# The last sixteen gate tiles of an input projection as eight pairs of seven block products

## The reference

```python
u = x @ w_in[l]
ua, ub, uc, ug = _split(u, GROUP_COLS)
oa, oc = _gdn_branch(ua, ...), _swa_branch(uc, ...)
ob, v_first = _rwkv7_branch(ub, x, ...)
gates = jax.nn.sigmoid(ug).reshape(bsz, t, N_BRANCH, d)
merged = (gates[:, :, 0] * (oa @ w_branch_a[l]) + gates[:, :, 1] * (ob @ w_branch_b[l])
          + gates[:, :, 2] * (oc @ w_branch_c[l]))
x = _layer_norm(ALPHA * x + merged @ w_out[l], ln1_w[l], ln1_b[l])
hid = jax.nn.silu(x @ ffn_gate[l]) * (x @ ffn_up[l])
x = _layer_norm(ALPHA * x + hid @ ffn_down[l], ln2_w[l], ln2_b[l])
```

## Time and profile before

| | us |
|---|---|
| median of 3 runs | 1847.23 (1846.68 to 1847.53) |
| the profiled execution, its own time | 1851.59 |
| its span | 1849.8 |
| PE busy | 1811.3 |
| DVE busy | 1139.0 |
| ACT busy | 670.3 |
| POOL busy | 591.2 |
| granted clock, mean | 0.992 |

### The profile page before, as it was taken

The page is one execution under the profiler, slowest core; times in us unless marked ns, Lnnn a source line. Parts: engine busy times, 40 slices in busy tenths (PEclk is TensorE's granted clock), DMA queues, the critical chain, the costliest instruction groups (busy, mean ns, idle before and its releaser), DMA issues. The chain is left out here.

```text
span 1849.8 us, 28784 instructions
## 1 busy us (share of the span) xinstructions
PE 1811.3 (98%) x11396; PEld 1488.5 (80%) x11396; DVE 1139.0 (62%) x1347; ACT 670.3 (36%) x1140; POOL 591.2 (32%) x420
## 2 busy tenths in 40 slices
PE   7999999999999999999989999999999999999997
PEld 6878888777788888788878778888888888888885
DVE  3757675666309940377768653966566666565586
ACT  3444434244421112266652131243333333444241
POOL 1211222211123322344415452765555554500000
PEclk9999999999999999999999999999999999999998
DMA  6245675225673377377755473234545445488563
GB/s 175 49 88 136 150 183 140 73 73 145 164 199 92 93 164 223 115 214 222 206 191 191 132 236 109 82 98 154 189 135 157 151 163 185 150 277 301 179 213 132
DMA packets 383030, 292.76 MB, mean 158 GB/s; under 512 B 170764, under 2 KB 314764, under 8 KB 380848
## 3 DMA queue, kind: packets, MB, share of 16 engines
q1 hardware_dynamic: 307472, 237.14, 43.4%
q10 hardware_dynamic: 75424, 53.78, 10.4%
HBM read 195.84 MB, written 94.98 MB: 157 GB/s over the span
## 5 line engine op out<-in xcount | busy, mean ns | idle before, releaser
L158 PE MATMUL bank<-xhi,w_hi 128*128 128x512 f32 x976 | 385.8, 395 | 5.8 <-POOL w_lo L446 2.7
L160 PE MATMUL bank<-xhi,w_lo 128*128 128x512 f32 x976 | 381.0, 390 | 0.0
L159 PE MATMUL bank<-xlo,w_hi 128*128 128x512 f32 x976 | 380.5, 390 | 0.0
L446 POOL TENSOR_TENSOR w_lo<-w_raw,w_hi 128x1024 fp32r<-128x1024 f32 x61 | 169.2, 2774 | 572.2 <-ACT w_hi L813 572.2
L158 PEld LDWEIGHTS bank<-xhi,w_hi 128*128 128x128 f32 x976 | 183.6, 188 | 47.8 <-issue 7.3
L160 PEld LDWEIGHTS bank<-xhi,w_lo 128*128 128x128 f32 x976 | 183.5, 188 | 39.4
L159 PEld LDWEIGHTS bank<-xlo,w_hi 128*128 128x128 f32 x976 | 183.8, 188 | 37.0
L1931 POOL TENSOR_TENSOR ff_ring_lo<-ff_w_sums,ff_ring_hi 128x512 fp32r<-128x512 f32 x88 | 127.6, 1451 | 73.7 <-ACT ff_ring_hi L2210 73.5
L1931 POOL TENSOR_TENSOR ff_ring_lo<-ff_raw,ff_ring_hi 128x512 fp32r<-128x512 f32 x66 | 95.9, 1455 | 149.6 <-ACT ff_ring_hi L2210 149.5
L799 ACT ACTIVATE work<-bank 128x512 f32<-128x512 f32 x70 | 42.0, 600 | 264.1 <-PE bank L160 256.3
L165 PE MATMUL b_ps<-x1hi,ff_ring_hi 128*128 128x512 f32 x264 | 103.0, 390 | 0.0
(11 more groups left out here) (410 smaller groups left out, 3984.1 us busy)
## 6 DMA issues: line engine op xcount, KB each, us to landing
w_raw<-in_w_in ACTq DMA_DIRECT2D x61, 512.0 KB, 4.4
hid_ops<-y SPq DMA_DIRECT2D x77, 256.0 KB, 2.8
ff_raw<-hid_ops SPq DMA_DIRECT2D x77, 256.0 KB, 3.8
op<-opnd SPq DMA_DIRECT2D x16, 1152.0 KB, 5.5
u<-work ACTq DMA_DIRECT2D x68, 256.0 KB, 4.3
b_gate<-u SPq DMA_DIRECT2D x24, 512.0 KB, 4.0
ff_raw<-in_ffn_gate SPq DMA_DIRECT2D x22, 512.0 KB, 4.2
ff_raw<-in_ffn_up SPq DMA_DIRECT2D x22, 512.0 KB, 6.0
```

What stands on the lines that cost most here:

```text
L158: pe.matmul(out, w_hi, x_hi, start=first, stop=False)
L159: pe.matmul(out, w_hi, x_lo, start=False, stop=False)
L160: return pe.matmul(out, w_lo, x_hi, start=False, stop=last)
L446: pool.tensor_tensor(w_lo[b][:, :, :], w_raw[b][:, :, :], as_f32(w_hi[b][:, :, :]), ALU.subtract).then_inc(w_lo_done, 1)
```

## The change

The last 16 of the 61 tiles, all of them gates, are no longer computed tile by tile. They form eight pairs; a pair with the two halves of the channels and the two halves of the frames is a 2x2 by 2x2 block product, done by Winograd's form of Strassen's method in seven products of blocks in place of eight. A product is 4 channel blocks by three matmuls of 128x512.

- The seven products take sums of blocks. Sums of the tokens are made once (`t1` to `t4`, four blocks each): two of them by POOL between the last seven ordinary tiles, one by DVE before the pairs' fifth product, one by DVE near the end. Each sum is split again into a high part (ACT) and a low part. Sums of the weights are made by POOL for every pair (`pair_sum`), and a high and a low part for each of the products (`pair_high` on ACT, `pair_low` on POOL).
- Six products of each pair come one after the other (`PAIR_ORDER`), their sums accumulate in PSUM or are added by DVE (`add_u2`, `add_rest`); the partial result that waits for the seventh goes to a DRAM buffer `hold` or stays in SBUF. The seventh products of all pairs follow as a second pass (`second`), with `last_add` on DVE. Sigmoid and store are ACT's.
- Both raw tiles of a pair have one buffer; the next pair is loaded (`load_pair`) when the third low part of the pair is done.
- The inversion starts with the RWKV blocks alone, 44 steps, while the last GDN blocks are still on their way; then the parts alternate. Between its steps stand DVE's sums for the pairs, at fixed step numbers (`STEPS_BEFORE`).
- Before the scan only chunks 0 and 1 are loaded; chunk 2 is loaded at the beginning of the scan, since its tiles' space is used for token sums.

The core of the diff (8 columns of indentation cut off):

```diff
-    NT_IN = len(ORDER)
+    NT_IN = len(ORDER) - 2 * PAIRS
     NQ = 2 * NT_IN
-    at_tile = {row: m for m, row in enumerate(ORDER)}
+    G, NP1 = PAIRS, 6 * PAIRS
+    PAIR_ORDER = (1, 6, 2, 7, 5, 3)
+    SECOND = (G - 2, G - 1, *range(G - 2))
...
+t1 = [x_of(k, 1) for k in range(4)]
+t2 = list(zip(in_raws[0:4], (*in_raws[4:6], t2_low_up[:, :], t2_turned[:, :])))
+t3 = [(pieces(t3_tile, HALF * k), pieces(t3_tile, HALF * (4 + k))) for k in range(4)]
...
+x_part = {1: [x_of(k, 0) for k in range(4)], 2: [x_of(4 + k, 0) for k in range(4)], 3: [x_of(4 + k, 1) for k in range(4)],
+          4: t2, 5: t1, 6: t2, 7: t3}
+w_slot = lambda w, n: w[(NT_IN + n % 4 // 2) % 2][:, n % 2 * 4:n % 2 * 4 + 4, :]
...
-inv_n, inv_x, inv_xt, prod = of_blocks(8), of_blocks(11), of_blocks(0), of_blocks(14)
+inv_n, inv_x, inv_xt, prod = of_blocks(8), of_blocks(11), of_blocks(8), of_blocks(14)
 R = NPAIR // 2
 PARTS = (slice(0, 2), slice(2, R))
-INV_STEPS = 2 + 2 * (NB - 1)
+INV_STEPS, ALONE = 2 + 2 * (NB - 1), 44
+STEPS_BEFORE = (70, 72, 76, 78, 86, 88, 104, 106, 115, 117, 123, 125)
...
+    def sum_t2(k):
+        out, (bh, bl), (dh, dl), (ah, al) = t2_sum[k], x_of(k, 1), x_of(4 + k, 1), x_of(k, 0)
+        if k == 0:
+            pool.wait_ge(conv_done, 12)
+        if k == 3:
+            pool.wait_ge(turn_stored[0], 16 * turn_count[0])
+        step(pool.tensor_tensor(out, as_f32(dh), as_f32(bh), ALU.subtract))
...
+        summed(pool.tensor_tensor(out, out, as_f32(al), ALU.add), ("t sum", k))
...
+    def sum_t3(k):
+        out, (th, tl), (ah, al) = t3_sum[k], t2[k], x_of(k, 0)
+        if k == 0:
+            for b in range(2):
+                pool.wait_ge(g_stored[b], 96)
+            pool.wait_ge(mm_done, max(turned_by("gdn", i, n) for i in range(GH) for n in "vk"))
+            pool.wait_ge(sums_made, made["t lo", 3])
...
+    def pair_sum(g, p):
+        a11, a12 = (flat4(raw_of(0, kh)) for kh in range(2))
+        a21, a22 = (flat4(raw_of(1, kh)) for kh in range(2))
+        a, b, how = {5: (a21, a22, ALU.add), 6: (s_sums[5], a11, ALU.subtract), 7: (a11, a21, ALU.subtract), 3: (a12, s_sums[6], ALU.subtract)}[p]
+        if p == 5:
+            pool.wait_ge(p_landed, 32 * g + 48)
+        if g:
+            pool.wait_ge(w_lo_done, NT_IN + 6 * (g - 1) + PAIR_ORDER.index(p) + 1)
+        if p == 6:
+            pool.wait_ge(sums_made, made["weight", g, 5])
+        if p == 3:
+            pool.wait_ge(sums_made, made["weight", g, 6])
+        summed(pool.tensor_tensor(s_sums[p], a, b, how), ("weight", g, p))
...
+    first = NT_IN - 7
+    sums = {first: [(sum_t2, 0)], first + 1: [(sum_t2, 1), (low_t, 0)], first + 2: [(sum_t2, 2), (low_t, 1)], first + 3: [(sum_t2, 3), (low_t, 2)],
+            first + 4: [(low_t, 3), (sum_t3, 0), (sum_t3, 1)], first + 5: [(low_t, 4), (low_t, 5), (sum_t3, 2), (sum_t3, 3)], first + 6: [(low_t, 6), (low_t, 7)]}
     for m in range(NT_IN):
         b = m % 2
         pool.wait_ge(w_hi_done, m + 1)
         pool.tensor_tensor(w_lo[b][:, :, :], w_raw[b][:, :, :], as_f32(w_hi[b][:, :, :]), ALU.subtract).then_inc(w_lo_done, 1)
+        for do, k in sums.get(m, ()):
+            do(k)
+    for g in range(G):
+        if g == 0:
+            pair_sum(0, 5)
+            pair_sum(0, 6)
+        n = 6 * g
+        pair_low(n)
+        pair_low(n + 1)
+        pair_sum(g, 7)
+        pair_sum(g, 3)
+        for k in range(2, 5):
+            pair_low(n + k)
+        if g + 1 < G:
+            pair_sum(g + 1, 5)
+            pair_sum(g + 1, 6)
+        pair_low(n + 5)
+    for i in range(G):
+        pair_low(NP1 + i)
...
+            else:
+                sp.wait_ge(nt_stored, 480)
+                for r in range(2):
+                    for pp in range(2):
+                        sp.dma_start(inv_n[64 * pp:64 * pp + 64, r, :, :], nt[2 * r + pp].rearrange("c b s t -> (c b) s t")).then_inc(inv_landed, 16)
...
+    load_chunk(sp, 0, early, opnd, xinv, early_landed, early_inv)
+    sp.wait_ge(early_landed, 112)
+    sp.wait_ge(early_inv, 48)
+    sp.wait_ge(p_held, 16 * (G - 1))
+    sp.wait_ge(w_lo_done, NT_IN + NP1)
+    sp.wait_ge(p_add, add_at(G - 1, 3))
+    for i in range(2, 5):
+        sp.dma_start(second_piece[i], hold[SECOND[i]]).then_inc(p_back, 16)
+    sp.wait_ge(p_add, add_at(G - 1, 5))
+    sp.dma_start(second_piece[5], hold[SECOND[5]]).then_inc(p_back, 16)
+    sp.wait_ge(mm_done, N_MM + NP1)
+    load_chunk(sp, 1, early, opnd, xinv, early_landed, early_inv)
...
+    def product(n):
+        g, p = n // 6, PAIR_ORDER[n % 6]
+        to = pair_bank[g % 2][X_AT[p]]
+        pe.wait_ge(w_lo_done, NT_IN + n + 1)
+        if p == 1:
+            if g == 0:
+                pe.wait_ge(g_norm_done, GH)
+                pe.wait_ge(masked, 16)
+            elif g == 1:
+                pe.wait_ge(evac, len(ITEMS))
+            else:
+                pe.wait_ge(p_read, snap_at(g - 2) + 1)
+        elif p == 2:
+            pe.wait_ge(p_read, snap_at(g))
+        elif p == 6 and g >= 2:
+            pe.wait_ge(p_add, add_at(g - 2, 5))
+        elif p == 3:
+            pe.wait_ge(p_add, add_at(g, 1))
+        for k in range(4):
+            if g == 0 and p in (6, 7):
+                pe.wait_ge(sums_made, made["t lo", 4 * (p - 6) + k])
+            if g == 0 and p == 5:
+                pe.wait_ge(p_add, edge_lo_at(0, k))
+            last = more_dot(pe, to, w_slot(w_hi, n)[:, k, :], w_slot(w_lo, n)[:, k, :], *x_part[p][k], p != 2 and k == 0)
+        last.then_inc(mm_done, 1)
...
+    def high_t1(k):
+        act.wait_ge(p_add, edge_sum_at(0, k))
+        act.activation(t1[k][0], t1_sum[k], ACT.Copy).then_inc(t_hi, 1)
...
+    def load_pair(g):
+        act.wait_ge(w_lo_done, NT_IN)
+        if g:
+            act.wait_ge(w_lo_done, NT_IN + 6 * g - 3)
+        for i in range(2):
+            col = in_column(gate_row(g, i))
+            act.dma_start(w_raw[i][:, :, :], w_rows[:, :, col:col + P]).then_inc(p_landed, 16)
...
+    high_after = {2 * (NT_IN - 6 + k): (k,) for k in range(4)}
+    high_after[NQ - 4], high_after[NQ - 2] = (4, 5), (6, 7)
...
+            for n in high_after.get(q, ()):
+                high_t(n)
+            if q == NQ - 3:
+                load_pair(0)
+            if q >= NQ - 2:
+                pair_high(q - (NQ - 2))
     store_u(NQ - 2)
+    high_t1(0)
     finish(NQ - 1)
+    pair_high(2)
     store_u(NQ - 1)
+    high_t1(1)
+    pair_high(3)
...
+    for j in range(NP1 + G):
+        act.wait_ge(mm_done, N_MM + j + 1)
+        g, p = j // 6, PAIR_ORDER[j % 6]
+        if j < NP1:
+            if p == 1:
+                act.activation(snap, pair_bank[g % 2][0], ACT.Copy).then_inc(p_read, 1)
+                if g + 1 < G:
+                    load_pair(g + 1)
+            if p == 2:
+                pair_out(g, 0)
+        if j + 4 < NP1 + 4:
+            pair_high(j + 4)
+        elif NP1 < j < NP1 + G - 3:
+            pair_high(j + 3)
+        if j < 2:
+            high_t1(j + 2)
...
+    def make_t1(_):
+        dve.wait_ge(mm_done, done_at[NQ - 2])
+        dve.wait_ge(sums_made, made["t sum", 3])
+        for k in range(4):
+            out, (hi, lo), (ah, al) = t1_sum[k], t1[k], x_of(k, 0)
+            step(dve.tensor_tensor(out, as_f32(lo), as_f32(al), ALU.subtract))
+            step(dve.tensor_tensor(out, out, as_f32(hi), ALU.add))
+            dve.tensor_tensor(out, out, as_f32(ah), ALU.subtract).then_inc(p_add, 1)
+            if k:
+                low_t1(k - 1)
...
+    def add_u2(g):
+        if g:
+            dve.wait_ge(p_add, add_at(g - 1, 5))
+        dve.wait_ge(mm_done, N_MM + 6 * g + 2)
+        dve.wait_ge(p_read, snap_at(g))
+        dve.tensor_tensor(u2, pair_bank[g % 2][1], snap, ALU.add).then_inc(p_add, 1)
...
+    todo = [(make_t1, 0)]
+    for g in range(G):
+        todo += [(add_u2, g)] + ([(make_t4, 0)] if g == G - 1 else []) + [(add_rest, g)]
+    todo += [(last_add, i) for i in range(G)]
+    parts, done, turn_at = [steps(part) for part in PARTS], [0, 0], list(STEPS_BEFORE)
+    for n, k in enumerate((0,) * ALONE + (1, 0) * (INV_STEPS - ALONE) + (1,) * ALONE):
+        while turn_at and turn_at[0] <= n:
+            turn_at.pop(0)
+            do, at = todo.pop(0)
+            do(at)
+        if done[k]:
+            dve.wait_ge(inv_step[k], done[k])
+        else:
+            dve.wait_ge(inv_landed, (64, 32 * R)[k])
+        next(parts[k]).then_inc(inv_step[k], 1)
+        done[k] += 1
...
+            for u_stored, count in u_last:
+                sp.wait_ge(u_stored, count)
+            load_chunk(sp, 2, tiles, opnd, xinv, landed[2], inv_landed[2])
```

More of the change, by code:

```diff
@@ L316, in project_and_prepare @@
     raw_use, seen = {}, [0, 0, 0]
-    for row in ORDER:
+    for row in ORDER[:NT_IN]:
         if row in RAW_SLOT:
@@ L402, in project_and_prepare, with summed @@
         inv_step = [sem(f"inv_step{k}") for k in range(2)]
-        block = local.open_block()
```

(69 more changed lines are left out.)

226 lines of the change are left out of this document (185 added, 41 removed).

## The result

The changed kernel takes 1895.24 us (median of 4 runs, 1894.26 to 1896.27), the kernel before 1846.95 beside it: 1.0266 times as long, interval 1.0253 to 1.0279. That is 48.3 us more where +32.7 was forecast, and less than half a microsecond beyond the range (1847.2 x 1.0266 = 1896.4, the range ended at 1896). The sign was right, and it lies where the forecast put it; the size was not right.

What follows compares the result with a forecast made beforehand. PE bounds the old kernel; after the change, POOL and DVE's serial chain holds PE. 782.6 + 1.2 + 6 + 2.3 - 759.4 = +32.7 us, on 1847.2 gives 1880 us; range 1837 to 1896 for 8 in 10.

Steps and rivals of the forecast that it cites:

- Matmuls, 21.8 us saved: Last sixteen tiles on PE: 672 matmuls in place of 768, at 0.2267 us each, 21.8 us less.
- POOL and DVE exclude each other: Projection: POOL sums and DVE instructions with two SBUF inputs run one after the other, whole instruction by whole instruction.
- The serial sum, 199.3 us from 518, and 6 idle: Until the sixth pair's second product: POOL's 122.1 plus DVE's 77.2 us run serially, to 717.3; about 6 us with neither running.
- Clock at 0 in a chain that POOL holds: PE's lower clock after stalls, mostly covered by POOL's chain: taken as 0, at most 2.5 us in each of five stalls.
- After 717.3 come 24 products, 65.3 us, and two load loops 1.2: From the sixth pair's second product to PE's end: 65.3 us of products plus 1.2 us for weight loads, nothing else.
- rival D: PE's clock drops in each stall uncovered: forecast plus 12, 1892 us; chance counted within the forecast's 0.68.
- Inversion's way out at nothing: Inversion's stores and chunk 0's load after its end near 728 us: done ahead of PE's 790, no cost.
- Boundary 2.3: From PE's last product to the scan: DVE add, four memsets, ACT's sigmoid and store beside them, 2.3 us.
- A: Rival: POOL late only by its own work, DVE's work falling into POOL's waits: 9.1 us gained, 1838 us; chance 0.13.
- C: Rival: half of the POOL and DVE collisions count, 38.6 us instead of 77.2: 1840 to 1862 us; chance 0.11.
- B: Rival: PE stays the bound and everything is hidden: 19.5 us gained, 1828 us; chance 0.08.
- The collision's 45 us: At the sixth pair's second product: serial POOL and DVE work reaches 717.3 us, PE alone 672.4; the collision costs 45 us.

Runs made afterwards that it cites:

- experiment 1: Two runs on the changed kernel: the inversion's 62 products cut to one element per block, 1859.18 us; its 62 reductions cut so instead, 1891.69 us.
- experiment 4: Changed kernel plus matmuls with overwritten results before PE's waits: two waits past 720 us, 1894.73 us; or those at tiles 42 to 44, 1895.82 us.
- experiment 3: Changed kernel, with SP loading the scan's chunk 0 only when the last pair's weights have landed: 1887.40 us.
- experiment 6: Changed kernel, chunk 0 loaded after the last pair's weights, plus: POOL's sixth low part earlier, 1885.88; second-pass loads early, 1883.65; these and overwritten matmuls, 1884.76 us.
- small products: Changed kernel with the block inversion's 62 products taking one element of each block, reductions whole: 1859.18 us.
- experiment 4's tail: Changed kernel plus 37 matmuls with overwritten results before PE's waits at 744.7 and 773.9 us: 1894.73 us.
- first repair of four pairs: Four-pair kernel (1852.83 us) with chunk 1 loaded right behind the last product, token low parts one tile later, 12 overwritten matmuls: 1851.34 us.
- early loads: Changed kernel with chunk 0 loaded after the last pair's weights, and the second pass's loads of tiles 5 to 7 issued early: 1883.65 us.
- second repair: On top of the first repair of four pairs, chunk 0's load waits until the second pair's weights have landed: 1847.50 us.
- experiment 5: Changed kernel with POOL's 32 chained token sums in the last seven ordinary tiles done by DVE instead: 1884.03 us.

## Why the prediction was wrong, by its steps

- *Matmuls, 21.8 us saved:* right. PE keeps 0.2267 us from start to start except at the lower clock behind a wait, and the page of the profile counts 96 fewer.
- *POOL and DVE exclude each other:* right in the main, and shown (experiment 1): 36 us hang on the products alone.
- *The serial sum, 199.3 us from 518, and 6 idle:* right as a date, by two errors that cancel. The first step came at 514.13 us (518.3 in the forecast's time). The sixth pair's first sum was forecast at 723.3; it came at 720.66, which is 724.9. It was 1.6 us short. DVE in order of time (the second row is the last product):

```profile
720.66 0.68 DVE L1482 TENSOR_TENSOR work<-bank,work 128x512 f32<-128x512 f32 x1
721.37 1.97 DVE L1440 TENSOR_TENSOR work<-work 128x961 f32<-128x961 f32 x1
```

But of these 206.5 us (514.13 to 720.66), added up from both engines' rows, some 16 have neither POOL nor one of DVE's products, its copy or token sums in them, where 6 were taken; the longest piece is the 3.4 us in which POOL waits for ACT's high part of a token sum at 594.3, and five more, 0.9 to 1.8 us each, lie at POOL's waits for weights and high parts. In the other 190 at least one of them ran, where 199.3 was due, although POOL had by then done 59 of the pairs' operations and not 54. So the exclusion is a little less than whole: from 523.17 to 530.05 us POOL's chained sums start 1.6 to 1.8 us apart in place of 1.36 (588.03 to 590.75, without a product beside them), 0.3 to 0.5 more, for a product each that alone would take 0.6 to 0.9 (an estimate from the products of 50 and 128 elements, 0.26 and 0.41 us). That 10 us too little idle time met 9 us too much work was luck.

- *Clock at 0 in a chain that POOL holds:* nothing speaks against it up to there. The granted clock was 0.91, and taking the slow starts behind two of three stalls away bought nothing (experiment 4).
- **"After 717.3 come 24 products, 65.3 us, and two load loops 1.2": this step failed, by 15.1 us.** From 720.66 to the last product's end (802.06 + 0.23) it is 81.6 us. 65.3 are products, 10.3 idle (5.8, 2.8 and 0.3, 1.5) and 6.0 slow clock. The 5.8 are the last pair's weights beside chunk 0's load, the 1.5 a load beside chunk 1's. The forecast priced chunk 0 only as "done ahead of PE's 790", thus by when it ends, and didn't ask what it delays. 2.8 is DVE's chain of 16 operations for the seventh products' tokens, which can start only when the last pair's second product is done; the forecast didn't price it, and it wasn't repaired here. The clock's 6.0 stand in PE's own rows, in the stage for which the forecast took nothing, and rival D had its price in the stalls before. Experiments 3 and 6 take 11.6 of the 15.1 back; of the clock's 6.0 only the part behind the load stall is in that (experiment 3 gave 7.8 us for 5.8 of idle time, the one sign that it counts), the rest was not separated.
- *Inversion's way out at nothing:* the stores and the landing were in time; what was missing is the line above.
- *Boundary 2.3:* 2.95 against 1.63 us, so 1.3 more. The forecast's sum counts all 2.3 as new, from PE's end in the kernel before, although that kernel already spends 1.63 there. *Scan at nothing:* right, 1088.7 us both times.

Together 32.7 + 1.6 + 15.1 - 1.0 = 48.4, measured 48.3.

**The range.** Its end at 1896 isn't the sum of the upper ends that the forecast names: with 9 us more of idle time, 2.7 at the boundary and 12.5 for the clock it is 1880 + 24.2 = 1904. The clock was left out of it.

**Rivals.** A and C are out by experiment 1. B's bound, the lateness at tiles 43 and 44, shows with small products as 3.1 us at one tile. Of what was to show the forecast, POOL's share (83%) and the waits before sixth products came; POOL's operations were at 1.70 and not near 2 us, since many meet a reduction or nothing, and DVE bears the other half of the collision (its products 93.6 us for 74.4 in the earlier trace rows). The waits at tiles 43 and 44 were 11.4 us, and one at tile 42 had 5.1. "Little idle after the inversion's end" was wrong: a fifth of that stage was lost.

The collision's 45 us stand for 77 us of DVE's work. Small products take away 66 of these, 38.6 us by proportion, and 36 were gained; what the other 11 (DVE's token sums for the fifth products) cost was not run by itself. Nor is the clock's share behind 720 us settled: in each comparison made something later took the gain up, in whole or in part (a load in experiment 4, SP at the edge in experiment 6), and what is left is within the runs' spread.

## What to carry to other kernels

Before POOL is given work as a free engine, add its time and that of DVE's instructions with two SBUF inputs into one sum, and hold it against PE's time for the same stretch; a pair saves 2.7 us of PE and adds 9.4 us of POOL (ten operations and the seventh's low part, less two of the old ones). Put such work where DVE has none of them (four pairs behind the inversion gave 42 of the 48 us back, where half as many pairs alone would give 24). A transfer off the critical path is priced by which load it travels beside, not only by when it is due, and for a stall that no other engine's chain covers the slow clock after it is an upper end to keep in the range.

## What the runs showed of the hardware

- A load of a pair's weights (512 KB) beside a chunk's transfers took up to 10.5 to 12.2 us to land (the changed kernel 11.6, experiment 4's tail 12.2, the first repair of four pairs 10.5). In the kernels that keep the chunk away from them it was 5.5 to 7.6 us (experiment 3 6.9, the early loads 7.6, the second repair 5.5). The second pass's seventh load, half as large as one of these, was put to use 11.6 us after its issue beside chunk 1's (experiment 4).
- In the changed kernel 6 to 13 starts 0.42 to 0.43 us apart followed each idle time of 1.85 us and more in front of the scan (1.7 to 3.0 us lost), and none followed those of 1.5 us and less. The length of the idle time alone doesn't settle it: none followed idle times of 1.87 and 3.55 us in experiment 5 and one of 2.60 with the early loads. With thrown-away matmuls in the gap the starts stayed near 0.23 (experiment 4's tail, granted clock 1.00 from 776 to 784 us).
- A short DVE product suffers most for its size: the one of 128x162 took 1.58 us (519.38 us) where the one of 128x128 before it took 0.41. A POOL operation ran from 519.35 to 520.64; 0.32 us behind its end the product was done, so it waited for the whole of it.
